# Two output projections' norms run beside the projection that follows, the double norm staggered by a step per tile, and loads moved into the scan before them

## The reference

```python
def hybrid_layer(h, hc, ...):
    lat = split_cols((rms_norm(h, norm_g) * (1.0 + scale) + shift) @ w_in)
    ...
    y = jnp.concatenate([y_conv, att_l * g_att, hg_l * g_hg, y_four], axis=-1) @ w_out
    h_new = h + gate * y
...
def first_block(...):
    for layer in range(DEPTH):
        h, hc = hybrid_layer(h, hc, ...)
    return rms_norm(h, final_g)
...
def second_block(x, ...):
    modulate(rms_norm_2(x, mix_pre_norm[l]), mod_x[0], mod_x[1]) @ w_in[l]
    ...
    ssd_x = ssd_finish(y_x, xs_x, z_x, ssd_d[l], ssd_norm[l])
    mix_x = jnp.concatenate([attn_x, ssd_x], axis=-1) @ w_out[l]
    x = x + mod_x[2] * rms_norm_2(mix_x, mix_post_norm[l])
```

## Time and profile before

| what | us |
|---|---|
| median of three runs | 4219.2 |
| the profiled execution | 4214.63 |
| its span | 4212.8 |
| TensorE busy | 3772.8 (90%) |
| VectorE busy | 2658.5 (63%) |
| ScalarE busy | 1964.8 (47%) |

### The profile page before, as it was taken

The page is one execution under the profiler, slowest core; times in us unless marked ns, Lnnn a source line. Parts: engine busy times, 40 slices in busy tenths (PEclk is TensorE's granted clock), DMA queues, the critical chain, the costliest instruction groups (busy, mean ns, idle before and its releaser), DMA issues. The chain is left out here.

```text
span 4212.8 us, 57691 instructions
## 1 busy us (share of the span) xinstructions
PE 3772.8 (90%) x21712; PEld 2916.6 (69%) x21712; DVE 2658.5 (63%) x4019; ACT 1964.8 (47%) x3612; POOL 959.1 (23%) x1088
## 2 busy tenths in 40 slices
PE   6989888988899787986889999989987999999998
PEld 5775677777675565765656666677755777888886
DVE  3756467967666477966555555546976666666655
ACT  4544255445454275444434444445543554444444
POOL 0017002630006102600045655600093000101000
PEclk7999999989999898998999999999999999999999
DMA  5100113565200111033100000022001652111244
GB/s 185 41 16 1 47 41 110 204 217 180 76 28 1 52 41 51 2 107 101 30 5 6 5 10 5 21 82 77 11 6 61 221 175 55 41 61 40 105 150 145
DMA packets 211398, 295.98 MB, mean 70 GB/s; under 512 B 74218, under 2 KB 140010, under 8 KB 211124
## 3 DMA queue, kind: packets, MB, share of 16 engines
q1 hardware_dynamic: 210564, 292.09, 20.9%
q0 software_dynamic: 416, 0.05, 0.0%
q10 hardware_dynamic: 144, 0.15, 0.0%
HBM read 261.65 MB, written 30.51 MB: 69 GB/s over the span
## 5 line engine op out<-in xcount | busy, mean ns | idle before, releaser
L570 DVE TENSOR_TENSOR x_low<-buf_a,x_high 128x640 fp32r<-128x640 f32 (+5 forms) x360 | 357.6, 993 | 399.1 <-ACT x_high L536 396.4
L536 ACT CAST x_high<-buf_a 128x640 fp32r<-128x640 f32 (+5 forms) x360 | 310.9, 864 | 503.4 <-PE ps L601 433.2
L599 PE MATMUL ps<-x_high,w_high 128*128 128x512 f32 (+1 forms) x1184 | 449.9, 380 | 94.4 <-DVE w_low L574 88.0
L600 PE MATMUL ps<-x_low,w_high 128*128 128x512 f32 (+1 forms) x1184 | 438.2, 370 | 0.0
L601 PE MATMUL ps<-x_high,w_low 128*128 128x512 f32 (+1 forms) x1184 | 438.0, 370 | 0.0
L3172 PE MATMUL ps<-w_high,x_high 128*128 128x512 f32 x896 | 362.0, 404 | 74.2 <-DVE w_low L3000 70.4
L3174 PE MATMUL ps<-w_high,x_low 128*128 128x512 f32 x896 | 356.5, 398 | 0.0
L3173 PE MATMUL ps<-w_low,x_high 128*128 128x512 f32 x896 | 356.0, 397 | 0.0
L599 PEld LDWEIGHTS ps<-x_high,w_high 128*128 128x128 f32 x1184 | 227.6, 192 | 165.1 <-DVE x_low L570 110.7
L3000 DVE TENSOR_TENSOR w_low<-w,w_high 128x1024 fp32r<-128x1024 f32 x170 | 208.0, 1223 | 183.9 <-ACT w_high L3120 183.9
L3742 DVE TENSOR_REDUCE mx<-ps 128x1 fp32r<-128x1280 f32 x128 | 190.7, 1491 | 199.7 <-PE ps L3617 199.2
(11 more groups left out here) (446 smaller groups left out, 8889.1 us busy)
## 6 DMA issues: line engine op xcount, KB each, us to landing
w<-in_w_out SPq DMA_DIRECT2D x26, 2048.0 KB, 8.8
w<-in_w_mod SPq DMA_DIRECT2D x24, 2048.0 KB, 9.4
w<-in_w_down SPq DMA_DIRECT2D x15, 2048.0 KB, 7.9
w<-in_w_in SPq DMA_DIRECT2D x26, 1024.0 KB, 5.2
w<-in_w_up SPq DMA_DIRECT2D x22, 1024.0 KB, 7.6
w<-in_w_in SPq DMA_DIRECT2D x6, 2048.0 KB, 8.6
x<-in_x SPq DMA_DIRECT2D x16, 512.0 KB, 9.0
scratch_h<-x SPq DMA_DIRECT2D x8, 512.0 KB
```

The lines of the kernel that those rows point to most:

```text
L536: act.copy(xh[i % NX][:, 0:s["tn"]], x_of(s)).then_inc(x_high, 1)
L570: dve.tensor_tensor(xl[i % NX][:, 0:s["tn"]], x_of(s), xh[i % NX][:, 0:s["tn"]].bitcast(F32), ALU.subtract).then_inc(x_low, 1)
L599: pe.matmul(g["out"], lhs[0][:, :], rhs[0][:, :], start=(s["kk"] == 0), stop=False)
L600: pe.matmul(g["out"], lhs[0][:, :], rhs[1][:, :], start=False, stop=False)
```

## The change

- The first output projection's norm and layer 1's qkv projection become one block. The norm's last group (two tiles) is done in eight pieces beside the first eight steps of the qkv projection (`before` in `project_split`). Its six PSUM banks are taken in the order 4, 5, 0, 1, 2, 3. `NormRooms` places the norm's tiles in memory so that the projection can use what is spent.
- The same for the second output projection, with its double norm, and the raw projection.
- The double norm's pieces are staggered. At kk 1 the first tile's sum; at kk 2 its first scaling and the second tile's sum; at kk 3 its second scaling, the second tile's first scaling and the third tile's sum, and so on.
- In `ssd_scan` the tiles that lie in the weight slots are sorted by kind, one kind for each slot, so that one slot is free before the scan ends; the first weight chunk of the third projection and the first part of the attention result are loaded during the scan. The barrier at its end stays.
- In `project_split` jobs that are plain copies evacuate their first half by VectorE and the second by ScalarE, and the casts and subtractions of the two steps behind such a job are issued with its evacuations behind them on ScalarE, and between them on VectorE (`splits_at`).

The core of the diff:

```diff
-def project_split(k, jobs, *rooms, moves=(), beside=None, banks=8, leave=False):
+def project_split(k, jobs, *rooms, moves=(), beside=None, banks=range(8), leave=False, before=None):
...
+            plain = j["do"] == "copy" and "second" not in j and "silu_from" not in j
...
-                    by = "act" if do == "silu" or do == "copy" and len(groups) % 2 else "dve"
+                    late = len(mine) >= (len(subs) * len(toks) + 1) // 2 if plain else len(groups) % 2
+                    by = "act" if do == "silu" or do == "copy" and late else "dve"
...
+    def splits_at(i):
+
+        if i >= 2 and steps[i - 2]["last"] and steps[i - 2]["plain"]:
+            return []
+        return range(i, min(i + 1 + (i >= 1 and steps[i - 1]["last"] and steps[i - 1]["plain"]), len(steps)))
...
+            for i, s in enumerate(steps):
+                if before and i == before.STEPS:
+                    before.turned(dve, before.n_tiles)
+                    before.stores_done(dve)
+                for n in list(splits_at(i))[:1]:
+                    split(n)
+                if before and i < before.STEPS:
+                    before.dve(i)
+                evacuate(evacuations(i, "dve"))
+                for n in list(splits_at(i))[1:]:
+                    split(n)
+                if beside and i >= beside.first:
+                    next(parts, None)
...
+            for i, s in enumerate(steps):
+                if before and i == 0:
+                    act.wait_ge(ws.products, start)
+                    before.turned(act, (steps[0]["t0"] + steps[0]["tn"]) // P)
+                elif before and i == before.STEPS:
+                    before.turned(act, before.n_tiles)
+                    before.stores_done(act)
+                for n in splits_at(i):
+                    split(n)
+                if before and i < before.STEPS:
+                    before.act(i)
                 evacuate(evacuations(i, "act"))
...
+        def _(sp):
+            if before:
+                ws.load_until(sp, steps[0]["chunk"])
+                sp.wait_ge(ws.products, start)
+            if beside:
+                beside.load(sp)
+            ws.load_until(sp, steps[0]["chunk"])
+            if before:
+                before.sp()
...
+                    before.pe(i)
+                    if i == before.STEPS - 1:
+                        before.turned(pe, before.n_tiles)
...
+    if norm:
+        with k.joined():
+            project_split(k, jobs, Layout(k, lay.o, A_C), beside=heads, banks=(4, 5, 0, 1, 2, 3), before=norm())
+    else:
+        project_split(k, jobs, Layout(k, lay.o, A_C), beside=heads, banks=range(6))
...
+    following = k.ws.taken
+    of_slot = [slots[(following + i) % W_SLOTS] for i in range(W_SLOTS)]
+    xw, S, xd = ([[room(f"{n}{w}{i}", [P, D]) for i in range(2)] for w in range(2)]
+                 for n, room in zip(("xw", "s", "xd"), of_slot))
...
-            k.ws.load_until(sp, k.ws.taken)
+            sp.wait_ge(conv.activated, conv.TILES)
+            norm.load_first(sp)
+            sp.wait_ge(inc_ready, 4 * (U - 1))
+            k.ws.load_until(sp, following + 1 - W_SLOTS)
...
+class NormRooms:
+
+
+    def __init__(self, k, last, spent, small):
+        self.last, self.spent, self.small = (Layout(k, A_R + a * 1024, A_R + b * 1024) for a, b in (last, spent, small))
+
+    def __call__(self, name, shape, dt=F32):
+        if name.startswith(("x_", "w_", "gate_row1", "pre_row")):
+            return self.spent(name, shape, dt)
+        small = name in ("stat", "mod_cols", "gain_col", "gate_row0", "trash")
+        return (self.small if small else self.last)(name, shape, dt)
...
+    def load_part(self, sp, c):
+        chunks, whole = slice(c * KD // 2, (c + 1) * KD // 2), self.k.d["attn"].rearrange("(c p) t -> p c t", p=P)
+        sp.dma_start(self.attn[:, chunks, self.tokens[0]], whole[:, chunks, self.tokens[0]]).then_inc(self.attn_in[c], 16)
+
+    def load_first(self, sp):
+
+        self.load_part(sp, 0)
...
+        self.load_part(sp, 1)
+        weights(1)
...
+                elif pre is not None:
+                    if 3 <= kk <= 5:
+                        tile_of(scale, mine, kk - 3)
+                    if 2 <= kk <= 4:
+                        tile_of(norm_before, mine, kk - 2)
+                    if 1 <= kk <= 3:
+                        tile_of(add, mine, kk - 1)
+                    if kk >= 5:
+                        tile_of(transposes_out, mine, kk - 5)
...
-                elif kk == 3 and pre is not None:
-                    tile_of(scale, mine, 0)
-                    tile_of(add, mine, 1)
-                    tile_of(norm_after, mine, 2)
...
-                elif kk == 4 and pre is not None:
-                    tile_of(norm_before, mine, 1)
-                    tile_of(scale, mine, 1)
...
-                elif kk == 5 and pre is not None:
-                    tile_of(transposes_out, mine, 0)
-                    tile_of(add, mine, 2)
-                    tile_of(norm_before, mine, 2)
...
-                if kind == "pre":
-                    root(n, kind)
...
+                elif pre is not None:
+                    if 3 <= kk <= 5:
+                        tile_of(root_main, mine, kk - 3)
+                    if 2 <= kk <= 4:
+                        tile_of(root_pre, mine, kk - 2)
+                        tile_of(square_main, mine, kk - 2)
+                    if 1 <= kk <= 3:
+                        tile_of(square_pre, mine, kk - 1)
+                    if kk >= 5:
+                        tile_of(transposes_out, mine, kk - 5)
...
+        def first_norm():
+            return project_normalize(k, branches, KD, [tile(t, "ctx" if t < CT_ else "x", res=True, store=None if t < CT_ else "h1")
+                                                       for t in range(NT)],
+                                     GROUPS, XA, (3 * D, 4 * D), d["norm_g"][1], scratch(), 2 * D, leave=True)
...
+        mixer_layer(k, 1, XA, XB, first_norm)
+        second_block(k, XA, rows, tile, second_norm)
...
+        before = norm()
+        project_split(k, [raw_job(0, HALF, QL), raw_job(HALF, O2_Z - HALF + ND, 0)], Layout(k, A_B, A_R),
+                      banks=(4, 5, 0, 1, 2, 3, 6, 7), before=before)
```

More of the change, by code:

```diff
@@ L462, in project_split @@
                 ws.count += len(mine) if last else 1
-                steps.append(dict(job=j, fm=fm, kk=kk, chunk=c, t0=t0, tn=tn, groups=mine, last=last, after=ws.count))
+                steps.append(dict(job=j, fm=fm, plain=plain, kk=kk, chunk=c, t0=t0, tn=tn, groups=mine, last=last, after=ws.count))
                 if last:
@@ L1254, in recurrence_norm, with mixer_layer @@
     k.done(sems)
-def mixer_layer(k, layer, XT, YT):
+def mixer_layer(k, layer, XT, YT, norm=None):
     d = k.d
@@ L2820, in project_normalize @@
     elif pre is not None:
-        order = [("post", 0), ("pre", 0), ("main", 0), ("post", 1), ("post", 2), ("pre", 1), ("main", 1), ("pre", 2), ("main", 2)]
+        assert post is None
+        order = [(kind, j) for j in range(3) for kind in ("pre", "main")]
     else:
```

189 lines of the change are left out of this document (80 added, 109 removed).

## The result

The changed kernel took 4189.11 us (median of 4 runs, 4185.10 to 4190.22) against 4218.12 us before (4 runs, 4216.09 to 4220.19): a ratio of 0.9929, 95% interval 0.9916 to 0.9942, so 29 us faster where 33 to 34 were forecast (4185, range 4167 to 4206). The profiled execution took 4189.99 us with a span of 4188.1.

A forecast was written before the change was run, and what follows sets the result against it. TensorE, busy for 90% of the span, was taken as the bound, with time only in its waits and half-clock stretches. 10.7 + 9.1 - 1 + 7.5 + 7.5 = 33.8 off 4214.6, plus 4.6 for the median: 4185 us, range 4167 to 4206.

The forecast's parts named there:

- A: First output projection's norm beside the qkv projection: the stage boundary goes, 10.7 us gained (7 to 13).
- B2: Second output projection's double norm beside the raw projection's first steps: 9.1 us gained (5 to 13).
- B: Stagger of the double norm's scalings and squares beside matmuls: a loss of 1 us (-6 to +4).
- C: Scan to third norm: weights and attention part loaded during the scan, 7.5 us gained (4 to 11.5).
- D: Job boundaries of plain projections: next two steps' splits ahead of evacuations, 7.5 us gained (1 to 12).
- The term for the conv boundaries: Five boundaries of the x, B and C jobs: 0.9 us gained at each, 4.5 together.
- waits near 1 us: Sign that the forecast is right: TensorE waits of that length at the boundaries of the plain jobs.
- The raw projection's 0.5: Raw projection: 0.5 us gained by issuing splits ahead of evacuations.
- The term for the gates: Gates stages: splits ahead of evacuations gain 1.6 us in layer 1 and 1 in layer 0.
- The first rival: TensorE's clock stays down through the new waits: 41 lost against 34 gained, 7 to 8 us slower, 4227; 4%.
- The second rival: Squares dominate in the norm groups and tails: B costs 6, other parts bring less, 15 us gained, 4204; 15%.
- The third: Everything hides, as the chains of different tiles overlap in groups and tails: 52 us gained, 4167; 9%.

The follow-up runs named there:

- the kernel with overlapped squares: Changed kernel without splits ahead in the gates; double norm does the next tile's sum and first square ahead of this tile's second square: 4169.91 us (0.9886).

## Why the prediction was right, and where it was not

- **A, 10.7 forecast.** 9.9 and 11.1 in the two profiles, 10.1 with the part undone (6.9 by the medians). The start came 2.32 us behind the last matmul where 2.4 was reckoned, and the later waits were 1.72 and 1.31 where 0.35 to 1.5 stood. Right, and shown.
- **B2, 9.1 forecast.** 8.3 in the stage, and 5.3 of it with the join alone undone. That 9.1 came near is luck, by two errors that cancel. The waits were put at 13.1 and are 7.5, since I let two steps each carry 3.9 where only one carries 3.44. The slow stretch was put at 1.5, but at a clock of 0.73 over 31.3 us some 17 of them went by at half clock (twice 0.27 of the stretch), and what was computed in these took twice as long.
- **B, a loss of 1 forecast.** A gain of 0.7 beside matmuls; the loss is in the tail, 4.5 beside the raw projection, a place where I did not price the stagger apart from the join. The chains are what sets the waits, as the kernel with overlapped squares shows, but laid end to end they came out too long: 9.55 and 15.8 us of waits were reckoned for the two groups, 25.4 together, and 17.8 are measured.
- **C, 7.5 forecast.** 6.3 by the medians, 6.7 to 7.7 in the stage. The wait of 16.03 became 5.06, 2.71 and smaller ones, on z and then on the constants, as forecast.
- **D, 7.5 forecast: the step that failed.** It is worth 0.5 us by the medians, nothing that can be told. (Its four terms add up to 7.6.) The term for the conv boundaries, 4.5, counted waits alone. They shrank by 1.9 only: waits near 1 us were to be the sign, and of the five three are 1.65 to 1.68 and one is 2.60. The clock gave back more than that, so the gain in and behind the jobs is 5.9 against the kernel with the part undone and 9.1 against the one before; that the term is not far off is luck. The raw projection's 0.5 is not borne out: its start takes 93.8 us with the part undone and 94.7 with it. The term for the gates had the wrong sign: 2.6 gained were forecast and 6.2 to 6.6 lost, because I looked at the cast that was late before and not at what stands ahead of the cast after it. That explains layer 1, where the waits grew by 3.1; layer 0, with waits of like sum, lost by the clock, which the term did not price.
- **The first rival**, a clock that stays down through many short waits, did come true in part, 0.73 in the raw projection's start, and 0.86 in the qkv projection's in one of the two profiles; it costs some microseconds, not 41. The second rival is not borne out: 17.8 us of waits in the groups are less than the 19.5 before. The third was not this kernel but what the better order reached: 4169.91 against the 4167 that were given for it.

29 of the 33.8 forecast were found, then, with the missing 5 near the 7 that D didn't bring. That the whole came this near is in part luck, since errors of both signs went into it. The z projection's 2.9 us are lost in code that is the same in both kernels, which only comes at another time; there the half clock lasted the whole of the first 5.7 us in the changed kernel and half of them before (the first stretch is of the changed kernel, the second of the one before):

```profile
2741.90:2747.60 5.70, 5.69 (x14) 4.50 (x15) 2.19 (x5) 0.52 (x3) 0.00 (x0) 0.50 0.62 232
```

```profile
2753.20:2758.90 5.70, 5.70 (x19) 4.61 (x20) 2.79 (x7) 1.65 (x5) 0.00 (x0) 0.75 0.63 236
```

The Trainium skill (TensorE: Matmul & The Clock Gate, Part 1, "What's actually happening") says that a half-rate clock is the default and that activity releases it. The traces agree so far: the raw projection's start, with four waits in 31.3 us, shows 0.73, and the clock is back at 1.00 in the steady matmuls behind it. Which break brings half clock they do not tell.

Why the clock falls behind one wait of 2.0 us and not behind the next was not settled; no experiment moved a wait in time and changed nothing else. What the record does show is that neither the wait's length nor the code around it decides this by itself. The changed kernel was profiled twice, and at the qkv projection's start the same wait of 2.32 us was followed by half clock in the first profile and not in the second; the stage took 156.3 us in the first and 155.1 in the second. And in layer 0's gates a wait of 1.81 us in the changed kernel was followed by half clock, and one of 1.79 at the same matmul of the kernel with the first join undone was not, though the code there is the same:

```profile
1068.50:1071.90 3.40, 3.40 (x11) 2.80 (x10) 1.62 (x3) 0.57 (x1) 0.00 (x0) 0.50 1.03 334
```

```profile
1065.72 0.36 PE L639 MATMUL ps<-w_high,x_high 128*128 128x256 f32 x1 [2.32 <-DVE x_low L533]
...
1067.60:1071.00 3.40, 3.21 (x17) 2.48 (x16) 2.65 (x5) 1.25 (x2) 0.00 (x0) 1.00 1.07 335
```

```profile
583.55 0.36 PE L639 MATMUL ps<-x_high,w_high 128*128 128x256 f32 x1 [1.81 <-DVE w_low L537]
...
583.80:587.20 3.40, 3.40 (x12) 2.82 (x12) 2.84 (x3) 3.30 (x4) 0.00 (x0) 0.50 0.00 0
```

```profile
583.05 0.36 PE L639 MATMUL ps<-x_high,w_high 128*128 128x256 f32 x1 [1.79 <-DVE w_low L537]
...
583.30:586.70 3.40, 3.40 (x20) 2.91 (x20) 2.84 (x3) 3.31 (x4) 0.00 (x0) 1.00 0.02 5
```

That the stagger's 4.5 us in the tail are the clock alone rests on two granted clocks and like sums of waits, and was not tried by itself.

## What to carry to other kernels

Before an instruction is issued earlier, look at what it leaves behind: the next one of its kind now stands behind two pieces of other work instead of one. Where a norm is done beside matmuls, order its pieces so that one tile's square runs while another's scaling does, and count each chain from the first wait to the next cast. Price a wait of TensorE with the slow stretch that may come behind it, and measure a part in its own stage, between the same two matmuls, rather than by the whole time.

## What the runs showed of the hardware

- Waits of 1.25 to 2.32 us were followed by half clock at some places and not at others of the same length. Of the boundaries of the x, B and C jobs, it came behind three of five in the kernel before, and none in the changed kernel, where the longest wait was 2.60. The same wait in the same code, 2.32 us, was followed by it in one execution and not in the next. I had taken waits of up to 2.5 us as harmless.
- Stages that were not touched differ by 2 to 3 us from kernel to kernel, in steps: the z projection takes 97.8 to 97.9 or 100.0 to 100.8 us, the scan's last 150 matmuls 27.7 or 30.6. Each is read from one profiled execution of each kernel. So an edit's effect on the whole time can be off by that much, and by the whole time alone it can't be told from the edit's own.
